# Output projection of a two-layer decoder trunk: GpSimd's weight remainders and squares in another order

## What is computed

```python
for l in range(DEPTH):
    mod = c_act @ ada_w[l] + ada_b[l]
    sh1, sc1, g1, sh2, sc2, g2 = [m[:, None, :] for m in jnp.split(mod, 6, axis=-1)]
    h = rms_norm(x, norm1_g[l]) * (1.0 + sc1) + sh1
    x = x + g1 * token_mixer(h, ...)          # ends with  concat([att, hm]) @ w_out[l]
    h = rms_norm(x, norm2_g[l]) * (1.0 + sc2) + sh2
    x = x + g2 * conv_ffn(h, ffn_up[l], ffn_conv_w[l], ffn_conv_b[l], ffn_down[l])
return rms_norm(x, final_g)
```

## Time and profile before

| | us |
|---|---|
| median of 3 runs | 1475.78 (1475.23 to 1476.37) |
| the profiled execution | 1480.02 |
| its span, first to last instruction | 1478.2 |
| PE busy | 1424.7 (96%) |
| PE waiting for `w_lo` from L561, at L1573 | 2.8 in 2 waits |
| mean granted TensorE clock | 0.985 |

### The profile page before, as it was taken

The page is one execution under the profiler, slowest core; times in us unless marked ns, Lnnn a source line. Parts: engine busy times, 40 slices in busy tenths (PEclk is TensorE's granted clock), DMA queues, the critical chain, the costliest instruction groups (busy, mean ns, idle before and its releaser), DMA issues.

```text
span 1478.2 us, 17608 instructions
## 1 busy us (share of the span) xinstructions
PE 1424.7 (96%) x7099; PEld 1173.4 (79%) x7099; DVE 635.9 (43%) x1067; ACT 512.7 (35%) x679; POOL 650.2 (44%) x298
## 2 busy tenths in 40 slices
PE   5799999998999999999999999999999999999998
PEld 5688887867788888888877888787778888888886
DVE  5726457648545545542321563684523121121131
ACT  4322444542243333331132143445524333332111
POOL 0334325232555555545643423343264555454552
PEclk8799999999999999999999999999999999999999
DMA  9633110035166666664432321100022232332331
GB/s 366 196 89 100 58 58 29 1 131 183 57 181 189 184 194 192 182 202 168 132 114 61 115 85 59 58 1 1 29 86 86 86 112 88 92 108 80 102 104 57
DMA packets 181974, 163.20 MB, mean 110 GB/s; under 512 B 16037, under 2 KB 147589, under 8 KB 181893
## 3 DMA queue, kind: packets, MB, share of 16 engines
q1 hardware_dynamic: 180724, 161.83, 34.7%
q10 hardware_dynamic: 1169, 0.25, 0.1%
HBM read 159.96 MB, written 2.10 MB: 110 GB/s over the span
## 4 chain that ended last, share of the span: by engine, by line
PE 81%; issue 6%; DVE 5%; POOL 3%; ACT 2%; POOLq 2%; DMA 1%; DVEq 0%; ACTq 0%; SPq 0%
PE psum L1573 19%; PE psum L1575 19%; PE psum L1574 19%; PE psum L1605 4%; PE psum L1606 4%; PE psum L1608 3%; PE psum L1892 2%; POOL w_lo L561 2%; PE psum L1614 1%; ACT w_hi L728 1%; PE psum L1757 1%; DVE psum L1069 1%; PE psum L1553 1%; PE psum L1878 1%; PE psum L1943 1%
## 5 line engine op out<-in xcount | busy, mean ns | idle before, releaser
L561 POOL TENSOR_TENSOR w_lo<-w_raw,w_hi 128x2048 fp32r<-128x2048 f32 x76 | 351.0, 4619 | 462.9 <-ACT w_hi L728 462.0
L728 ACT ACTIVATE w_hi<-w_raw 128x2048 fp32r<-128x2048 f32 (+2 forms) x104 | 192.9, 1855 | 608.0 <-PE psum L1575 472.2
L1573 PE MATMUL psum<-h_hi,w_hi 128*128 128x512 f32 x928 | 367.2, 396 | 3.7 <-POOL w_lo L561 2.8
L1575 PE MATMUL psum<-h_hi,w_lo 128*128 128x512 f32 x928 | 362.2, 390 | 0.0
L1574 PE MATMUL psum<-h_lo,w_hi 128*128 128x512 f32 x928 | 361.9, 390 | 0.0
L1573 PEld LDWEIGHTS psum<-h_hi,w_hi 128*128 128x128 f32 x928 | 174.8, 188 | 40.5 <-POOL w_lo L561 3.8
L1575 PEld LDWEIGHTS psum<-h_hi,w_lo 128*128 128x128 f32 x928 | 174.6, 188 | 36.9
L1574 PEld LDWEIGHTS psum<-h_lo,w_hi 128*128 128x128 f32 x928 | 174.7, 188 | 34.7
L566 POOL TENSOR_TENSOR w_lo<-w_raw,w_hi 128x1792 fp32r<-128x1792 f32 (+2 forms) x28 | 112.4, 4014 | 141.8 <-ACT w_hi L728 141.8
L1467 DVE SCALAR_TENSOR_TENSOR fy<-psum,par,fy 128x511 f32<-128x511 f32 x44 | 33.0, 750 | 269.3 <-ACT fy L928 269.3
L1573 PE MATMUL psum<-hid_hi,w_hi 128*128 128x512 f32 x352 | 137.8, 392 | 0.0
(11 more groups left out here) (270 smaller groups left out, 1916.0 us busy)
## 6 DMA issues: line engine op xcount, KB each, us to landing
w_raw<-in_ffn_up SPq DMA_DIRECT2D x88, 512.0 KB, 5.0
a_raw<-in_ada_w SPq DMA_DIRECT2D x56, 512.0 KB, 4.6
w_raw<-in_w_in SPq DMA_DIRECT2D x48, 512.0 KB, 4.4
w_raw<-in_ffn_down SPq DMA_DIRECT2D x32, 512.0 KB, 4.3
w_raw<-in_w_out SPq DMA_DIRECT2D x16, 512.0 KB, 4.3
a_raw<-in_ada_w SPq DMA_DIRECT2D x6, 1024.0 KB, 6.5
a_tok<-in_ada_w SPq DMA_DIRECT2D x6, 1024.0 KB, 7.1
w_raw<-in_ffn_down SPq DMA_DIRECT2D x16, 384.0 KB, 3.1
```

Of the source, the lines that this page charges most:

```text
L561: g.tensor_tensor(w_lo[:, slot_of(l, u), :], w_raw[:, slot_of(l, u), :], w_hi[:, u % HI, :].bitcast(F32), ALU.subtract).then_inc(s_lo, 1)
L728: s.activation(w_hi[:, u % HI, 0:n], w_raw[:, r, 0:n], ACT.Copy).then_inc(s_hi, 1)
L1573: m(ps, l_hi, r_hi, start=first, stop=False)
L1575: return m(ps, l_lo, r_hi, start=False, stop=last)
```

## The change

In each iteration of POOL's loop the remainder of unit 16+q is made ahead of the squares of that quarter instead of behind them.

```diff
                 for q in range(4):
+                    if q < 3:
+                        low(l, 16 + q)
                     for c8 in (2 * q, 2 * q + 1):
                         if c8 < KD - 2:
                             square(KD + 2 * KD * l, 2 * l + 1, c8)
-                    if q < 3:
-                        low(l, 16 + q)
                 low(l, 19)
```

## The result

The changed kernel takes 1482.95 us (median of 6 runs, 1480.27 to 1485.63) against 1476.76 for the kernel before in the same comparison (6 runs, 1475.23 to 1477.43). The ratio is 1.0044, with a 95% interval of 1.0033 to 1.0055: 6.2 us slower. The direction was forecast; the size was not, and 1482.95 lies above the range. Of the 2.65 us by which it passes the forecast of 1480.3, 1.0 is the kernel before, which took 1476.76 here and 1475.78 in the runs that the forecast went on, and 1.7 is the change. The profiled execution took 1482.40 us, its span is 1480.7.

What follows compares the result with a forecast made beforehand. PE was taken to bound the kernel, made late by POOL's order. Layer 0's -1.2 + 1.4 and layer 1's +3.0 + 1.3 gave +4.5 us on 1475.8, so 1480.3 us, range 1477.5 to 1482.0.

Steps and rivals of the forecast that it cites:

- What bounds the kernel: PE bounds; POOL's order delays it in layer 0, DVE is next; layer 1's sum has 2.9 us of slack.
- Layer 0, gain 1.2: Layer 0's output projection: quarter 3 starts at 375.85 instead of 377.07, held by DVE, a gain of 1.2 us.
- Layer 0's clock, 1.4: Behind a new 3.1 us pause ahead of layer 0's transposes, a 1.2 GHz stretch costs 1.4 us (0.7 to 1.6).
- Layer 1's wait, 3.0: At layer 1's sum PE waits for POOL's squares, delayed by unit 18's remainder, at a cost of 3.0 us.
- Layer 1's clock, 1.3 with an upper bound of 1.7: Behind layer 1's wait, one 1.2 GHz stretch on nine wide matmuls costs 1.3 us (1.0 to 1.7).
- The sum: Both layers' waits and clock losses together: +4.5 us on the median 1475.8, so 1480.3 us, 0.3% slower.
- The slow clock lasts longer: Rival: a second slow stretch follows behind a pause, another 1.6 us, +6.1 or 1481.9 us; chance 0.09.
- The rival in which the clock stays: Clock stays at 2.4 GHz through both pauses, only the waits count: +1.8 us, 1477.6 us; chance 0.12.
- The pauses that I leaned on: Trace pauses of 1.85 and 1.61 us were followed by 3.40 us at 0.50; those of 1.45 and 1.39 were not.

Runs made afterwards that it cites:

- a4: Kernel before with only unit 17's remainder moved ahead of the squares, units 16 and 18 behind as before: 1474.63 us against 1476.36, ratio 0.9995.
- c3: The kernel of a4 timed again, only unit 17's remainder ahead, against the kernel before: 1474.25 us against 1476.02, ratio 0.9990.
- b1: The change plus 13 unused wide matmuls on PE in layer 1 where it would wait for the squares: 1478.95 us, ratio 1.0017 to the kernel before.
- a2: The new order in layer 1 alone, layer 0 as in the kernel before: 1482.33 us against 1476.28, ratio 1.0042.
- c4: The changed kernel itself, nothing altered, profiled once more: 1484.29 us in that execution.
- c1: a4 plus the sum of POOL's squares behind the last matmul group at three of four norms: 1473.07 us, ratio 0.9981 to the kernel before.

## Why the prediction was right in direction and wrong in size

- **What bounds the kernel: right.** POOL's order made PE late in layer 0, DVE's products were next, and layer 1 had 2.9 us of slack at the sum and no wait to remove.
- **Layer 0, gain 1.2: right.** Quarter 3 was to start 0.41 behind the start of the second transposes, and did (372.17 to 372.58). PE stood 2.97 us ahead of them (forecast 3.1). Where the clock did not fall (a4) the gain shows by itself: 1.26.
- **Layer 0's clock, 1.4: right.** One stretch of 3.41 us begins between 0.5 us ahead of the pause's end and 1.0 behind it in all nine profiles that have it. In the eight of them that ask for the sums where the change does, it costs 1.3 to 1.7 us against a4 and c3, where the clock did not fall, and layer 0 as a whole changes by +0.1 to +0.4 where +0.2 was forecast.
- **Layer 1's wait, 3.0: right.** 2.97, and b1, which keeps the wait's cost but no idle time, has +3.1 in layer 1's span.
- **Layer 1's clock, 1.3 with an upper bound of 1.7: wrong, and this is the step that failed.** It priced one stretch and counted the nine wide matmuls alone. The clock stayed at 0.50 for 10.24 us and took the sums, the clock-keeping matmuls and the spreading with it: 3.9 us in the profile of the change (13.74 - 9.86), and 4.4 in a2 and c4 (53.65 and 53.62 - 46.27 - 2.97). The median of the change's runs leaves 2.9 for it, also above 1.7. Why the clock stayed low that long is open.
- **The sum.** With 3.9 in the place of 1.3 the forecast of +4.5 becomes +7.1, which is what the two spans of the profile give (0.3 + 6.8). The median of the runs, +6.2, lies somewhat below; the runs differ by 5 us among themselves. Seen as a difference, +6.2 is the upper end of the range (1482.0 - 1475.8), which reached that far for the rival with a second slow stretch; the 1.0 us that the kernel before took longer here put the time itself outside.
- **The rivals.** "The slow clock lasts longer" is what came, at +6.1 and 0.09. Its argument was there (sums of one column are little work), but I weighed it by the one stretch that layer 0 had shown, where a row of 24 wide matmuls follows. The rival in which the clock stays, at 0.12, did not come: it fell behind each of the nine pauses of 3.0 in layer 0, and in four of five profiles in layer 1. The Trainium skill (page "TensorE: Matmul & The Clock Gate", section "Why this matters for your kernels") sets a limit to idle gaps between bursts of matmuls, and these pauses of 2.97 us lie about at it. They were not safe here: a stretch at 0.50 came with 13 of 14.
- **The pauses that I leaned on** were a weaker sign than I took them for: 1.85 is followed by no stretch at 0.50 in a2, nor 1.86 in a4, c3 and c1, and the pause of 1.61, which all fourteen profiles have, is followed by one only in that of the kernel before. That trace also has two stretches of 3.41 us at 0.50 which the prediction did not weigh, from 297.70 and 307.94, with no idle time of PE over 0.8 us in the 5 us ahead of either. So a long pause was not the only thing that came ahead of a low clock.

## What to carry to other kernels

When a queue's order is turned around, ask of what moved back who asks for it and with how much slack: here 2.9 us of slack met a remainder of 4.6 us. A pause of PE cost 1.3 to 1.7 us for the clock ahead of 39 wide matmuls and 3.9 to 4.4 ahead of short matmuls and a chain of small steps. With 24 wide matmuls ahead of that chain it cost about 3 us in most runs, so that the kind of work decides is not shown; but price the clock over all that follows, and not over one stretch. And of three moves that look alike, try each by itself: unit 17's gains 1.2 us in layer 0's profile (timed again, -1.5 us, interval -2.7 to -0.1), unit 16's with it joins two pauses into one that costs the clock and gives the gain back, and unit 18's lost 6 us.

## What had not been expected of the hardware

- The pause of 2.97 us ahead of layer 1's sum was followed by 10.24 us at 0.50 (three times), and with 24 wide matmuls behind it by 6.83 us in one execution and none in another of the same kernel.
- Matmuls of one column slow down with the clock too: eight of them take 0.95 us at 1.00 and 1.70 at 0.50.
- Two pauses of 1.86 and 1.53 us, 13 us apart, left the clock at 1.00 in a4, and so did the like in a2, c3 and c1.
